# A streaming-encoder layer with 32 experts: the weight ring of nine places becomes one of eight from expert 6 on, with all its loads in pairs

## What is computed

```python
# x: (1, 256, 1024) float32
h = rmsnorm(x)
q, k, v, u, gate_a, gate_s = split(h @ w_in)
x = x + (sigmoid(gate_a) * attention(q, k, v) + sigmoid(gate_s) * glu(s5_ssm(u))) @ w_out
h = rmsnorm(x)                                   # 256 tokens
gate = softmax(top_4(h @ w_router + b_router))   # 4 of 32 experts for each token
for e in range(32):                              # rows routed to expert e
    gu = h_e @ w_up[e] + b_up[e]                 # w_up[e]:   (1024, 2048), 8 MB
    act = (clip(gu[:, 1024:], -7, 7) + 1) * g * sigmoid(1.702 * g)   # g = min(gu[:, :1024], 7)
    x += gate * (act @ w_down[e] + b_down[e])    # w_down[e]: (1024, 1024), 4 MB
x = x + sigmoid(rmsnorm(x) @ w_ple_gate) * rmsnorm(p @ w_ple_proj)
```

## Time and profile before

| | us |
|---|---|
| median of 3 runs | 1165.38 (1165.26 to 1166.26) |
| the profiled execution | 1164.75 |
| its span | 1162.9 |
| PE busy in it | 1119.2 (96%) |
| 16 DMA engines, queue of SP, share of the span | 90.1% |
| bytes moved | 441.04 MB, mean 379 GB/s |

### The profile page before, as it was taken

One profiled execution on the slowest core, in us unless ns is written; L12 is line 12 of the kernel. 1 busy time (PEld: TensorE's weight loads), 2 busy tenths in 40 slices (PEclk: granted clock), 3 DMA queues, 4 the chain that ended last, 5 costly groups with the idle time before them and its releaser, 6 DMA issues.

```text
span 1162.9 us, 15815 instructions
## 1 busy us (share of the span) xinstructions
PE 1119.2 (96%) x6541; PEld 496.1 (43%) x6541; DVE 387.8 (33%) x815; ACT 177.9 (15%) x304; POOL 153.5 (13%) x160
## 2 busy tenths in 40 slices
PE   9999999999999999999999999999999999999998
PEld 4587887533334333333333333333333333333344
DVE  6547858432223222212232222222222222222226
ACT  2372012320001000000211110101010101111113
POOL 2995664100000000000000000000000000000005
PEclk9999999999999999999999999999999999999999
DMA  9932346999999999999999999999999999999991
GB/s 308 380 97 80 139 164 261 372 420 422 427 428 431 427 438 431 428 433 433 425 435 433 428 436 431 425 437 433 426 433 433 427 435 432 428 437 424 427 421 47
DMA packets 40863, 441.04 MB, mean 379 GB/s; under 512 B 9796, under 2 KB 10368, under 8 KB 23040
## 3 DMA queue, kind: packets, MB, share of 16 engines
q1 hardware_dynamic: 40240, 439.01, 90.1%
q0 software_dynamic: 480, 1.57, 0.4%
q10 hardware_dynamic: 112, 0.02, 0.0%
HBM read 439.54 MB, written 1.05 MB: 379 GB/s over the span
## 4 chain that ended last, share of the span: by engine, by line
PE 62%; DMA 36%; DVE 1%; issue 1%; ACT 0%; SPq 0%; DVEq 0%
PE bank L1863 20%; DMA ring<-in_w_down_dram 18%; DMA ring<-in_w_up_dram 17%; PE bank L1917 12%; PE bank L1508 7%; PE bank L1525 4%; PE bank L1934 3%; PE bank L1680 2%; PE bank L1688 2%; PE bank L1827 2%; PE bank L1728 2%; PE bank L2039 1%; PE bank L1900 1%; PE bank L1971 1%; PE bank L1594 1%
## 5 line engine op out<-in xcount | busy, mean ns | idle before, releaser
L1863 PE MATMUL bank<-ring,arena 128*64 128x512 f32 x2040 | 452.8, 600 | 16.4 <-DMA ring<-in_w_up_dram 16.2
L1863 PEld LDWEIGHTS bank<-ring,arena 128*64 128x64 f32 x2040 | 143.7, 138 | 320.0 <-issue 290.8
L1917 PE MATMUL bank<-ring,arena 128*64 128x512 f32 x1024 | 231.9, 606 | 16.3 <-DMA ring<-in_w_down_dram 14.8
L1302 DVE TENSOR_TENSOR arena<-arena,bank 128x512 f32<-128x512 f32 x128 | 79.5, 682 | 289.1 <-PE bank L1934 289.1
L1917 PEld LDWEIGHTS bank<-ring,arena 128*64 128x64 f32 x1024 | 74.7, 139 | 152.9 <-issue 143.3
L1278 DVE TENSOR_SCALAR arena<-bank 128x512 f32<-128x512 f32 x32 | 22.1, 692 | 350.8 <-PE bank L1863 350.8
L648 POOL TENSOR_TENSOR ring<-ring 128x2048 f32<-128x2048 f32 x1 | 4.5, 4544 | 911.0 <-DMA ring<-in_w_ple_gate_dram 911.0
L838 ACT ACTIVATE arena<-arena 128x512 f32<-128x512 f32 x32 | 20.2, 630 | 493.4 <-DVE arena L1278 493.4
L1508 PE MATMUL bank<-arena,ring 128*128 128x256 f32 x384 | 86.4, 382 | 0.0
L1508 PEld LDWEIGHTS bank<-arena,ring 128*128 128x128 f32 x384 | 71.9, 190 | 12.6 <-issue 3.5
L1934 PE MATMUL bank<-arena 64*128 64x512 f32 x256 | 63.5, 614 | 0.0
(11 more groups left out here) (285 smaller groups left out, 794.6 us busy)
## 6 DMA issues: line engine op xcount, KB each, us to landing
ring<-in_w_up_dram SPq DMA_DIRECT2D x40, 4096.0 KB, 33.2
ring<-in_w_down_dram SPq DMA_DIRECT2D x24, 4096.0 KB, 34.9
ring<-in_w_up_dram SPq DMA_DIRECT2D x43, 2048.0 KB, 22.0
ring<-in_w_down_dram SPq DMA_DIRECT2D x15, 2048.0 KB, 15.9
ring<-in_w_in_dram SPq DMA_DIRECT2D x7, 2048.0 KB, 18.5
ring<-in_w_up_dram SPq DMA_DIRECT2D x9, 1024.0 KB, 21.0
ring<-in_w_glu_dram SPq DMA_DIRECT2D x2, 2048.0 KB, 8.3
ring<-in_w_out_dram SPq DMA_DIRECT2D x2, 2048.0 KB, 7.7
```

The lines of the kernel that those rows point to most:

```text
L1302: dve.tensor_tensor(part, part, bank[at][:, :], ALU.add).then_inc(m["sc_add"], 1)
L1863: last = pe.matmul(to, XS[:, k, :], columns, start=False, stop=(k == DT - 1))
L1917: last = pe.matmul(bank[YB][HALF * c:HALF * (c + 1), :], ACTT[:, j, HALF * h:HALF * (h + 1)], piece[:, j, 512 * c:512 * (c + 1)], start=(h ...
```

## The change

- The ring has nine places for the pieces of experts 0 to 5 and eight (`EVEN`) for those of experts 6 and up; the ninth is not used for weights after expert 5. `spot` counts from expert 6 anew.
- `left` waits, from expert 6 on, for the piece eight numbers before; a pair then waits for the piece seven before its first.
- All loads of experts 6 to 29 are pairs. Those of experts 3 to 5 are pairs too, but for one (expert 4's pieces 2 and 3, which go around the end of the nine).
- TensorE's and SP's loops have six rounds of four experts, 6 to 29 (24 pieces, three times around eight places). Experts 3 to 5 are written out ahead of the loop on both.
- The embeddings are ahead of expert 14 in place of 12. `XT3` moves to the ninth place.

```diff
-        FIRST, PERIOD = 3, 3
-        LAST = FIRST + 9 * PERIOD
-        ASIDE = FIRST + 3 * PERIOD
+        PAIRED, FIRST, PERIOD, EVEN = 3, 6, 4, 8
+        LAST = FIRST + 6 * PERIOD
+        ASIDE = FIRST + 2 * PERIOD
...
         def spot(n, c):
 
-            return (PER_EXPERT * n + c) % PLACES
+            return (PER_EXPERT * n + c) % PLACES if n < FIRST else (PER_EXPERT * (n - FIRST) + c) % EVEN
 
         def together(n, c):
 
-            return FIRST <= n < LAST and spot(n, c) < PLACES - 1
+            return PAIRED <= n < LAST and spot(n, c) < PLACES - 1
...
-        XT3 = place(spot(E - 2, 5))[:, 0:DT * SEQ].rearrange("p (k n) -> p k n", k=DT)
+        XT3 = place(PLACES - 1)[:, 0:DT * SEQ].rearrange("p (k n) -> p k n", k=DT)
...
             def left(n, c):
 
-                if c < 3:
-                    sp.wait_ge(READ[c + 3], n - 1)
+                back = PLACES - PER_EXPERT if isinstance(n, int) and n < FIRST else EVEN - PER_EXPERT
+                if c < back:
+                    sp.wait_ge(READ[c - back + PER_EXPERT], n - 1)
                 else:
-                    sp.wait_ge(READ[c - 3], n)
+                    sp.wait_ge(READ[c - back], n)
...
-            for i in range(PLACES, PER_EXPERT * FIRST):
+            for i in range(PLACES, PER_EXPERT * PAIRED):
                 n, c = divmod(i, PER_EXPERT)
                 load_piece(n, n, c)
-            for n in range(FIRST, FIRST + PERIOD):
-                for c in range(PER_EXPERT):
-                    left(n, c)
-                    counted = spot(n, c - 1) if c % 2 and together(n, c - 1) else spot(n, c)
-                    sp.dma_start(place(spot(n, c)), expert_source(n, c)).then_inc(arrived[counted], 16)
-            with sp.Fori(1, (LAST - FIRST) // PERIOD) as g:
+            for n in range(PAIRED, FIRST):
+                for c in range(0, PER_EXPERT, 2):
+                    load_pair(n, n, c)
+            with sp.Fori(0, (LAST - FIRST) // PERIOD) as g:
```

More of the change, by code:

```diff
@@ L288, in loads @@
                         last[n, c] = count[spot(n, c)]
-                    elif n < FIRST + PERIOD:
-                        count[spot(n, c - 1)] += 1
-                        last[n, c - 1] = count[spot(n, c - 1)]
             return last, count
```

## The result

| | before | after |
|---|---|---|
| median | 1164.92 us (1164.11 to 1166.26, 22 runs) | 1167.05 us (1165.5 to 1167.91, 22 runs) |
| ratio to before | | 1.0018 (95% interval 1.0012 to 1.0023) |
| span of the profiled execution | 1162.9 | 1165.2 |

The change makes the kernel 0.18% slower, 2.1 us. The forecast was 0.4 us faster, with a range of 1163.2 to 1167.0: by size the result is within 0.2%, but its sign is the other, and it lies just outside the range. The range was laid around the median of three runs, 1165.38; over 22 runs the kernel before is at 1164.92, so the change itself missed its forecast by 2.5 us.

A forecast was written before the change was run, and what follows sets the result against it. The unbroken stream of weights from expert 0 on was taken to set the end. Pairs gain 1.1 us, expert 3 loses 0.7: 0.4 less, 1165.38 to 1165.0 us, range 1163.2 to 1167.0.

The forecast's parts named there:

- The bound: From expert 0 on weights stream without a break; DMA idle time after 203 us costs as much at the end.
- What pairing is worth: 16 new pairs in experts 3 to 29 save 0.07 us each, 1.1 us gained; far bound 2.2.
- The rival of exposed starts: Each transfer's start is exposed and pairs halve the starts: 58 us gained (1107), or 32 us (1133); 1 in 100.
- The later waits at expert 3: Expert 3's first two pairs are issued late, leads 3.3 and 3.0 us: 0.7 us lost, bounds nothing to 1.6.
- losses don't add up and only the worst counts: At expert 3, a loss at the first pair delays its landing and gives the second more lead.
- the needed lead: Lead from issue to the previous landing that avoids loss at expert 3's pairs: at most 4.6 us.
- The piece whose lead of 3.6 I called free: Single piece issued early, at 249.10, in the kernel before; landed 4.9 after the one before, taken as no loss.
- Dry at every early pair: Rival: each of the eight new pairs of experts 3 to 5 loses 0.7 us, 5.6 in all; 1169.9; 5 in 100.
- Eight places: In the loop each pair waits 3.5 us longer, lead about 21 us, near 8 at experts 6 and 7: no cost.
- the embeddings: Moved two experts, they hold TensorE 12.7 us; lead behind them 11 to 12 us, or 9: costs nothing.
- the end: Experts 30 and 31 and `w_ple_gate` keep leads over 20 us; an earlier stream moves the end by as much.
- The loops are other code, not other work: The rewritten loops run the same matmuls, for which TensorE has time; no cost was counted.

The follow-up runs named there:

- one wait more: Kernel before with pairs in experts 3 to 5, expert 3's first two waiting for one piece more than needed: 1169.14 against 1164.69, ratio 1.0041.
- the pairs alone: Kernel before with the loads of experts 3 to 5 in pairs as its only change: 1166.58 against 1164.78, ratio 1.0015.

## Why the prediction was wrong

*The bound.* Right: the stream of weights ends the kernel, a step in the landings at 300 or 487 us is there to the end, and TensorE hides nothing of it. The rate is at 420 GB/s and more only from the ninth slice on; the eighth, which I counted in, is at 372. A second number was misread too. I gave TensorE's waits as 59.8 us, adding rows of its matmuls and of its weight loads. Ahead of `up` these are mostly the same waits seen twice. By matmuls alone they are 31.0 before, and after:

```profile
PEld bank L1859 <- DMA ring<-in_w_up_dram: 48.2, 22, 3.2
PE bank L1859 <- DMA ring<-in_w_up_dram: 29.4, 17, 2.3
PE bank L1913 <- DMA ring<-in_w_down_dram: 2.8, 7, 1.5
```

By matmuls alone these are 32.2, 1.2 more than before. By my adding they would be 80.4, and the forecast that they stay near 60 is wrong: nearly all waits now fall ahead of `up`, where the weight loads are counted too.

*What pairing is worth.* Right: 9.71 to 9.72 for each pair after. The rival of exposed starts falls with it. The Trainium skill's fit of a fixed 2.0 us for a DMA ("DMA: Bandwidth & Descriptors", "Anatomy of one DMA"), which I used there, is also for another path: the section gives it for transfers issued from GpSimd, and these are issued by SyncE.

*The later waits at expert 3.* The mechanism, the place, both issue times and, within 0.3 us, both leads were right. The term was mis-sized: 0.7 taken, 1.6 as its upper bound, 2.4 measured in the profile. The step that failed is the sentence that losses don't add up and only the worst counts. It took the needed lead, at most 4.6 us, as a fixed number that a delay at the first pair pays back at the second. In the changed kernel the 16 engines lost 0.9 us in the mean at the first pair and 1.4 at the second. Issued two at a time, single pieces lost 0.8 and 0.9; with one wait more the pairs lost 2.9 and 2.7. The losses add.

The needed lead isn't fixed either, as I counted it, from the last engine's landing: with one wait more a pair lost 2.9 at a lead of -0.5 (2.4 needed), and the next one 2.7 at a lead of 2.1 (4.8 needed). Counted from the first engine that was through with the transfer before, it is steadier. In all seven profiles with a short lead at expert 3 the first such pair or piece was issued between 0.9 us ahead of that moment and 3.0 us behind it, and the first engine's loss brings the need to 1.8 to 2.1 us each time. In the five of them with a second short lead the second needed 2.3 to 2.7. The piece whose lead of 3.6 I called free was issued 1.9 us ahead of that moment, and its first engine lost 0.3; the last engine, the one I looked at, lost nothing. I also passed over a late landing in those rows: the piece issued at 252.53 landed 5.4 after the one before, 0.5 late at a lead of 5.1. In the mean over the engines it lost 0.1, so this was one engine, behind a block of code fetched at 257 us, and not a queue run dry.

*The rival of that kind.* "Dry at every early pair" had the addition, and the wrong end: from the third pair on the queue didn't run dry, in the changed kernel or in the pairs alone, as its own condition said.

*Eight places, the embeddings, the end.* Right in what they cost: leads of 20 to 22 in the loop, 8.5 behind the embeddings (11 to 12 forecast, 9 allowed for), no loss; another place for the embeddings changes nothing.

*"The loops are other code, not other work."* This is the second step that failed. Code is a transfer too. Its price is 1.1 us by the median (0.0 to 2.1) for TensorE's three experts written out, as much as all 16 pairs gain, and 1.45 (0.8 to 2.9) for six. The instruction packets stood in the page before (22 of them), and no term was made of them. With 2.4 for the 0.7 at expert 3 and 1.1 for the code, the sum of the prediction becomes 2.4 + 1.1 - 1.1 = 2.4 us lost; 2.1 were measured.

## What to carry over

Where a queue of transfers sets the time, give each change of the ring its lead, issue to landing of the one before, at the place where the consumer is furthest behind. Look at the first engine to finish too, and not only at the last, which sets the landing. Keep single transfers there until the lead is long: here pairs with 5.1 us and more lost nothing for it, and pairs with 3.6 us and less did; short leads in a row add up. Merge transfers only where the queue is deep. And count code as traffic: written-out copies of a loop's body are fetched while the stream runs, and a gain of some hundredths of a microsecond for each transfer is easily less than that.

## What the runs showed that was not expected

The 16 engines don't finish a transfer together. By the semaphore's updates in the trace the first was 2.7 us ahead of the last in most of the kernel before. A transfer's landing is the last engine's, so a disturbance on an engine that is ahead costs nothing until it has used that up. In the changed kernel one engine fell back by 1.5 us behind the block of code at 480 us, and the spread grew from 2.9 to 4.2; the earlier blocks at 395 and 416 us put other engines back by as much, and those were ahead. That a block holds up one engine is read from these updates: the mean over the 16 is 0.1 us later behind each, a sixteenth of 1.5; that it is a different engine each time is inferred, since the trace doesn't name them.

TensorE's code was fetched in packets of 16 KB, and none came between 480 and 1083 us in the changed kernel: its loop of four experts stayed where it was after one round. The Trainium skill ("Runtime: NRT & Kernel Launch", "Terms") has an instruction memory of 32 to 128 KiB for each engine, refilled in blocks of 16 KiB; the trace agrees with the blocks' size on this queue (27 packets, 0.44 MB).

A starved queue costs more than the gap in it. The first packets behind one took up to 2.0 us (16 KB) and 2.7 us (32 KB) where a full queue's take 0.6 and 1.2. Why the second of two short leads needs more than the first, 2.3 to 2.7 us where the first needs 1.8 to 2.1, stays open.
